# Issuing the experts' down pieces from ACT's own DMA queue instead of SP's

## The chip, the core and the metric

The program runs on one core of a Trainium2 chip. The metric is device microseconds of one execution, the median of three runs. The engines named here are PE (TensorE, matrix products), DVE (VectorE), ACT (ScalarE), POOL (GpSimd) and SP (SyncE, which in this kernel only issues transfers). A transfer is issued by an engine on its queue, is carried by the core's 16 DMA engines, and tells by a semaphore that it has landed.

## The reference

A two-layer trunk on 256 tokens of 1024 floats. Layer 0 is a hybrid attention and a dense SwiGLU, layer 1 is a latent attention and a mixture of experts. Only the last part matters here:

```python
def moe_swiglu(h, w_router, w_gu, w_down):
    logits = (h @ w_router).astype(jnp.float32)
    vals, idx = lax.top_k(logits, TOP_K)                      # TOP_K = 2
    gates = jax.nn.softmax(vals, axis=-1)
    combine = jnp.sum(jax.nn.one_hot(idx, N_EXPERTS) * gates[..., None], axis=-2)
    y = jnp.zeros_like(h)
    for e in range(N_EXPERTS):                                # 8 experts
        y = y + combine[..., e:e + 1] * swiglu(h, w_gu[e], w_down[e])
    return y
```

An expert has a gate-and-up matrix of 1024 x 7168 and a down matrix of 3584 x 1024, all float32: 44.04 MB, eight times.

## The kernel before

The first 480 us or so are layer 0, the attention of layer 1 and the router. From there on the eight experts follow one another, seven in a loop and the last written out again behind it.

**The pieces.** The weights of an expert come in 42 pieces of 1 MiB, 128 partitions by 2048 floats. The list `EXP` (line 102) gives the order in which PE uses them. Its numbers are used throughout: 0 to 7 gate and up of set 0, 8 to 15 gate and up of set 1, 16 to 19 down of set 0, 20 to 27 gate and up of set 2, 28 to 31 down of set 1, 32 to 35 gate and up of set 3 (each as two transfers of 512 KB), 36 to 39 down of set 2, 40 and 41 down of set 3. So 28 pieces are gate and up ("gu") and 14 are down ("d").

**The homes.** A piece lies in one of 14 buffers, the homes; piece i goes to home i mod 14. The piece that follows in a home may be loaded when PE has used the one before it. PE adds one to the semaphore `used` (printed as pieces_used) with its last matmul of each piece, so piece i may be issued once piece i-14 is used up. SP does this for all pieces in the order of the list: wait for `used`, issue, next (lines 438 to 446, `fill` at line 388).

**PE.** For each piece PE waits for the home's semaphore (line 1820) and runs 12 matmuls of 32 tokens columns by 512 (24 in the trace, since each is two passes): line 1831 for gu, line 1839 for d. Between pieces stand short steps: the scatter of the expert before after piece 7 (line 1772), transposes of the activations after pieces 11, 23, 33 and 39 (line 1797), and the gather of the next expert's tokens after piece 39 (line 1764).

**ACT.** Its work in an expert, in the order in which it is written (`expert`, line 879):

- set 0: three tanh (line 883) when the sums of the set are there, the copy of the scatter matrix (line 889, waits for the scatter), then two copies of transposed activations (line 861)
- sets 1 and 2: three tanh, two copies each
- set 3: three copies of odd rows (line 895), three tanh (line 898), one copy (861), two copies of gathered tokens (line 855), three copies of the outputs' odd rows (line 908)

DVE makes the activations out of ACT's tanh (lines 1403, 1407, and for set 3 1415 to 1425), and PE's transposes wait for DVE, its d matmuls for ACT's copies at line 861.

Of the kernel before, what the change touches and what calls it, by code (L numbers as in the profile page):

```python
# [33 lines left out]
NE, FFE = 8, 3584  # L34
# [52 lines left out]
SETS = 3  # L87
# [14 lines left out]
EXP = expert_order()  # L102
NU = len(EXP)
HOMES = 14
# [25 lines left out]
HOME_OF = [14] + [(U0 - RING + i) % RING for i in range(RING)]  # L130
# [30 lines left out]
def build(nc, A):  # L161
# [3 lines left out]
    with ctx:  # L165
# [15 lines left out]
        homes = placed("homes", [P, 15, PIECE], f32, 0)  # L181
# [92 lines left out]
        used = sem("pieces_used")  # L274
# [81 lines left out]
        def expert_source(e, piece):  # L356
            kind, k, c = piece
            if kind == "d":
                r = k * 1024 + c * 2 * P
                return A["l1_exp_w_down"][e, r:r + 2 * P, :].rearrange("(p j) n -> p (j n)", j=2)  # L360
            n0 = k * 1024
            if k < SETS:
                return A["l1_exp_w_gu"][e, c * P:(c + 1) * P, :].rearrange("p (h n) -> p h n", h=2)[:, :, n0:n0 + 1024]
            return A["l1_exp_w_gu"][e, c * P:(c + 1) * P, :].rearrange("p (h n) -> p h n", h=2)[:, :, n0:n0 + COLS]

        def per(value, e, step):

            return value if e is None else e * step + value
# [9 lines left out]
        @block.sync  # L378
        def _(sp):
            def load(u, src, n):  # L380
                if u >= RING:

                    sp.wait_ge(lo_ready, u - RING + 1)
                c = src.shape[1]
                dst = ring[:, u % RING, 0:n].rearrange("p (c n) -> p c n", c=c)
                sp.dma_start(dst, src).then_inc(ring_loaded[u % RING], 16)

            def fill(i, e):
                kind, k, c = EXP[i]
                dst, there = homes[:, HOME_OF[i % HOMES], :], home_loaded[i % HOMES]  # L390
                if kind == "d":
                    sp.dma_start(dst, expert_source(e, EXP[i])).then_inc(there, 16)
                elif k < SETS:
                    sp.dma_start(dst.rearrange("p (h n) -> p h n", h=2), expert_source(e, EXP[i])).then_inc(there, 16)
                else:
                    for j in range(2):
                        sp.dma_start(dst[:, j * 1024:(j + 1) * 1024].rearrange("p (h n) -> p h n", h=2),
                                     expert_source(e, (kind, k, 2 * c + j))).then_inc(there, 16)

            for t in range(NT):  # L400
                sp.dma_start(x[:, t, :], A["x"][0, t * P:(t + 1) * P, :]).then_inc(x_loaded[t], 16)
            sp.dma_start(gain, A["l0_norm_attn"].partition_broadcast(P)).then_inc(gain0_loaded, 16)
            sp.dma_start(ident[:, :], A["ident"]).then_inc(ident_loaded, 16)
            for u, piece in enumerate(STREAM):
                if u == SLOTS:

                    for k, name in enumerate(("l0_a_q_norm", "l0_a_k_norm", "l0_b_q_norm", "l0_b_k_norm")):
                        sp.dma_start(raw_gains[:, k, :], A[name].partition_broadcast(P)).then_inc(tab_in, 16)  # L408
                    for t in range(NT):
                        sp.dma_start(rope[:, t, :], A["rope"][t * P:(t + 1) * P, :]).then_inc(tab_in, 16)  # L410
                    sp.dma_start(arena3[:, D + 256:D + 512],
                                A["l0_a_lambda"].rearrange("k d -> (k d)").partition_broadcast(P)).then_inc(tab_in, 16)
                    sp.dma_start(subln[:, :], A["l0_a_subln"].partition_broadcast(P)).then_inc(early_loaded, 16)
                    sp.dma_start(sinks[:, 0, :], A["l0_b_sinks"].partition_broadcast(P)).then_inc(early_loaded, 16)
                    sp.dma_start(rw[:, :, :], A["l1_router"].rearrange("(c p) e -> p c e", p=P)).then_inc(early_loaded, 16)
                load(u, piece_source(piece), piece_floats(piece))

            def first_fill(i):

                if i == 0:  # L420
                    sp.wait_ge(used, first(FFN) + len(FFN))
                elif i <= RING:
                    sp.wait_ge(lo_ready, U0 - RING + i)
                elif i <= RING + 2 * SLOTS:
                    sp.wait_ge(used, U0 - SLOTS + (i - RING - 1) // 2 + 1)
                else:
                    sp.wait_ge(routed, 1)
                fill(i, 0)

            def expert_pass(p):  # L430
                ub = U0 + p * NE * NU
                for i in range(HOMES):
                    if p:
                        fill(i, 0)
                    else:
                        first_fill(i)
                with sp.Fori(0, NE - 1) as e:
                    for i in range(HOMES, NU):
                        sp.wait_ge(used, per(ub + i - HOMES + 1, e, NU))
                        fill(i, e)  # L440
                    for i in range(HOMES):
                        sp.wait_ge(used, per(ub + NU + i - HOMES + 1, e, NU))
                        fill(i, e + 1)
                for i in range(HOMES, NU):
                    sp.wait_ge(used, ub + (NE - 1) * NU + i - HOMES + 1)
                    fill(i, NE - 1)

            def store(p):

                for q in range(4):  # L450
                    t, c = q // 2, slice((q % 2) * COLS, (q % 2 + 1) * COLS)
                    sp.wait_ge(scat_added, 4 * (NE + 1) * p + 4 * NE + q + 1)
                    sp.dma_start(A["out"][0, t * P:(t + 1) * P, c], x[:, t, c]).then_inc(stored, 16)
                sp.wait_ge(stored, 64 * (p + 1))

            expert_pass(0)
            store(0)
            sp.wait_ge(flag_ready, 1)
            most = sp.value_load(nmax_i[0:1, 0:1], min_val=0, max_val=SEQ)
            with sp.If(most > CAP):  # L460
                for p in range(1, PASSES):
                    expert_pass(p)
                    store(p)
# [103 lines left out]
        def _(a):  # L567
# [281 lines left out]
            def expert_pass(p):  # L849
                ub = U0 + p * NE * NU  # L850
# [22 lines left out]
                for b in range(4):  # L873
# [2 lines left out]
                                 bank(SCAT_BANKS[b])[0:CAP, :].rearrange("p (e n) -> p e n", e=2), ACT.Copy)\  # L876
                        .then_inc(scat_ready, 1)

                def expert(e, last):
                    for k in range(SETS):  # L880
                        for g in range(NG):
                            set_done(k, g, EXP.index(("gu", k, KC - 1)), e)
                            a.activation(gate[0:64, g, :], PS[0:64, g, :], ACT.Tanh, scale=0.5)\  # L883
                                .then_inc(gate_ready, 1)
                        if k == 0:

                            a.wait_ge(scattered, per(4 + 4 * (NE + 1) * p, e, 4))
                            a.wait_ge(scat_ready, 4 * p + 4)
                            a.activation(scatT[0:CAP, :], scatT_all[0:CAP, bass.ds(e, 1), :]
                                         .rearrange("p e n -> p (e n)"), ACT.Copy).then_inc(scatT_ready, 1)  # L890
                        copy_acts(2 * k, e, aT_pair, 6)
                        copy_acts(2 * k + 1, e, aT_third, 7)
                    for g in range(NG):
                        set_done(SETS, g, EXP.index(("gu", SETS, KC // 2 - 1)), e)
                        a.activation(gate[0:64, g, :], PS[64:P, g, :], ACT.Copy).then_inc(odd_copied, 1)  # L895
                    for g in range(NG):
                        a.wait_ge(set3_added, per(NG * NE * p + g + 1, e, NG))
                        a.activation(aux[0:GROUP, g, :], gate[0:GROUP, g, :], ACT.Tanh, scale=0.5)\
                            .then_inc(gate_ready, 1)
                    copy_acts(6, e, aT_last, 6)  # L900
                    if not last:
                        copy_tokens(2, e)
                    for g in range(NG):
                        if g < NG - 1:
                            a.wait_ge(y_summed, per((NG - 1) * NE * p + g + 1, e, NG - 1))
                        else:
                            a.wait_ge(used, per(ub + NU, e, NU))
                        a.activation(aux[0:64, g, :], PS[64:P, 3 + g, :], ACT.Copy).then_inc(y_odd, 1)  # L908
# [1003 lines left out]
```

## Time and profile before

| | |
|---|---|
| median of three runs | 1481.71 us (1478.5 to 1482.38) |
| the profiled execution, its own time | 1483.62 us |
| span of the profiled execution | 1481.8 us |
| mean granted clock of TensorE | 0.971 |
| PE busy | 1397.7 us, 94% |
| ACT busy | 344.2 us, 23% |
| moved by DMA | 415.97 MB, mean 281 GB/s |
| d piece from issue to landing, median | 6.8 us |
| gu piece of 1 MiB from issue to landing, median | 6.7 us |

The span is the time from the first to the last instruction. A matmul that is counted busy is in the pipeline; its record says when PE could start it and not how much of the array it used. DMA's share is that of the core's 16 DMA engines.

### The profile page before, as it was taken

The numbers are of one execution on the slowest core, as the hardware profiler recorded it, in microseconds if no ns is written. First come the engines' busy times: TensorE is split into PE (matmuls) and PEld (weight loads), VectorE is DVE, ScalarE is ACT, GpSimd is POOL, SyncE is SP. The second block draws the span as 40 slices with busy tenths as digits, with TensorE's granted clock in tenths as the row PEclk, the third lists the DMA queues.
The fourth block names the chain that finished last, engine by engine and source line by source line (L and its number), as shares of the span: only waits on it lengthen the run. The fifth ranks groups of instructions, "written<-read, shape, count | busy, mean of one in ns | idle before, by whom it ended". The sixth has DMA issues, their size and how long they took to land.

```text
span 1481.8 us, 25123 instructions
## 1 busy us (share of the span) xinstructions
PE 1397.7 (94%) x10702; PEld 687.6 (46%) x10702; DVE 479.8 (32%) x691; ACT 344.2 (23%) x603; POOL 65.9 (4%) x116
## 2 busy tenths in 40 slices
PE   5888899998788999999999999999999999999997
PEld 5667688887677433333333333333333332333332
DVE  3865555555753211221211221122121122121213
ACT  4355434433672101110200110111020111111011
POOL 3300000003500000000000000000000000000000
PEclk9988999999998899999999999999999999999998
DMA  9404455545216599999999989999989998999960
GB/s 311 159 14 133 148 165 194 175 169 153 101 64 237 222 351 387 350 345 386 358 349 375 391 321 362 388 347 352 378 342 352 388 380 320 378 388 349 359 259 31
DMA packets 117167, 415.97 MB, mean 281 GB/s; under 512 B 9152, under 2 KB 13632, under 8 KB 102592
## 3 DMA queue, kind: packets, MB, share of 16 engines
q1 hardware_dynamic: 116384, 412.25, 74.5%
q0 software_dynamic: 672, 2.03, 0.6%
q8 instruction: 95, 1.56, 0.4%
q14 instruction: 16, 0.13, 0.0%
HBM read 413.21 MB, written 1.05 MB: 280 GB/s over the span
## 4 chain that ended last, share of the span: by engine, by line
PE 88%; DVE 4%; ACT 2%; issue 2%; POOL 1%; SPq 1%; DMA 1%; POOLq 0%; DVEq 0%; ACTq 0%
PE PS L1831 39%; PE PS L1839 19%; PE PS L1454 6%; PE PS L1456 6%; PE PS L1455 6%; PE PS L1797 2%; PE PS L1772 2%; PE PS L1764 2%; PE PS L1562 1%; PE PS L1520 1%; ACT arena L631 1%; POOL stat L483 1%; DMA arena<-in_l_a_lambda 1%; PE PS L1706 1%; SPq L408 1%
## 5 line engine op out<-in xcount | busy, mean ns | idle before, releaser
L1831 PE MATMUL PS<-homes,tabs 128*32 128x512 f32 x5376 | 588.0, 593 | 9.6 <-issue 8.1
L1831 PEld LDWEIGHTS PS<-homes,tabs 128*32 128x32 f32 x5376 | 172.3, 110 | 400.1 <-issue 393.2
L1839 PE MATMUL PS<-homes,arena 128*32 128x512 f32 x2688 | 294.4, 592 | 0.6 <-ACT arena L861 0.6
L1403 DVE SCALAR_TENSOR_TENSOR arena<-arena,PS 64x512 f32<-64x512 f32 x72 | 49.0, 680 | 529.5 <-ACT arena L883 528.8
L1839 PEld LDWEIGHTS PS<-homes,arena 128*32 128x32 f32 x2688 | 86.5, 110 | 197.7 <-issue 196.3
L936 DVE TENSOR_TENSOR w_lo<-ring,w_hi 128x2048 fp32r<-128x2048 f32 (+2 forms) x56 | 123.9, 2219 | 106.5 <-ACT w_hi L580 94.7
L1454 PE MATMUL PS<-w_hi,hT_hi 128*128 128x512 f32 (+2 forms) x372 | 144.8, 389 | 14.0 <-DVE w_lo L936 10.1
L1455 PE MATMUL PS<-w_lo,hT_hi 128*128 128x512 f32 (+2 forms) x372 | 142.7, 384 | 0.0
L1456 PE MATMUL PS<-w_hi,hT_lo 128*128 128x512 f32 (+2 forms) x372 | 142.5, 383 | 0.0
L861 ACT ACTIVATE arena<-PS 128x512 f32<-128x512 f32 (+2 forms) x56 | 27.5, 491 | 444.9 <-PE PS L1797 444.3
L580 ACT ACTIVATE w_hi<-ring 128x2048 fp32r<-128x2048 f32 (+2 forms) x56 | 103.8, 1859 | 94.5 <-PE PS L1456 94.4
L883 ACT ACTIVATE arena<-PS 64x512 f32<-64x512 f32 x72 | 42.6, 591 | 303.9 <-PE PS L1831 303.9
L1454 PEld LDWEIGHTS PS<-w_hi,hT_hi 128*128 128x128 f32 x372 | 72.5, 195 | 29.5 <-DVE w_lo L936 11.8
L1456 PEld LDWEIGHTS PS<-w_hi,hT_lo 128*128 128x128 f32 x372 | 72.3, 194 | 13.0
L1455 PEld LDWEIGHTS PS<-w_lo,hT_hi 128*128 128x128 f32 x372 | 72.6, 195 | 12.4
L1432 DVE TENSOR_TENSOR arena<-arena,PS 32x512 f32<-32x512 f32 x48 | 32.6, 679 | 104.3 <-ACT arena L908 103.0
L1415 DVE TENSOR_TENSOR arena<-arena,PS 64x512 f32<-64x512 f32 x24 | 16.3, 679 | 143.9 <-ACT arena L895 143.9
L1407 DVE SCALAR_TENSOR_TENSOR arena<-arena,PS 64x512 f32<-64x512 f32 x72 | 49.7, 690 | 2.2
L1797 PEld LDWEIGHTS PS<-ident,arena 128*128 128x128 f32 (+2 forms) x224 | 31.1, 211 | 29.7 <-issue 26.8
L483 POOL TENSOR_TENSOR stat<-stat,neg_half 128x1 f32<-128x1 f32 (+4 forms) x24 | 33.2, 1388 | 153.4 <-DVE stat L964 146.1
L1797 PE MATMUL PS<-ident,arena 128*128 128x128 f32 (+2 forms) x224 | 38.6, 301 | 0.0
L1772 PE MATMUL PS<-arena 96*128 96x512 f32 x72 | 35.0, 631 | 3.3 <-DVE arena L1432 3.3
(186 smaller groups left out, 903.4 us busy)
## 6 DMA issues: line engine op xcount, KB each, us to landing
homes<-in_l_exp_w_gu SPq DMA_DIRECT2D x192, 1024.0 KB, 6.7
homes<-in_l_exp_w_down SPq DMA_DIRECT2D x112, 1024.0 KB, 6.8
homes<-in_l_exp_w_gu SPq DMA_DIRECT2D x64, 512.0 KB, 6.2
ring<-in_l_ffn_w_gu SPq DMA_DIRECT2D x22, 1024.0 KB, 5.2
ring<-in_l_ffn_w_down SPq DMA_DIRECT2D x11, 1024.0 KB, 4.9
ring<-in_l_w_in SPq DMA_DIRECT2D x9, 1024.0 KB, 11.0
ring<-in_l_w_out SPq DMA_DIRECT2D x4, 1024.0 KB, 5.1
ring<-in_l_c_w_out SPq DMA_DIRECT2D x4, 1024.0 KB, 5.1
```

What stands on the lines that cost most here:

```text
L483: pool.tensor_tensor(s, s, neg_half[:, 0:R_COLS[r]], ALU.pow).then_inc(rstd_ready, 1)
L580: a.activation(w_hi[:, u % SLOTS, 0:n], ring[:, u % RING, 0:n], ACT.Copy).then_inc(hi_ready, 1)
L936: v.tensor_tensor(w_lo[:, u % SLOTS, 0:n], ring[:, u % RING, 0:n], w_hi[:, u % SLOTS, 0:n].bitcast(f32), ALU.subtract).then_inc(lo_ready, 1)
L1403: v.scalar_tensor_tensor(out=act_of[g], in0=gate[0:64, g, :], scalar=1.0, in1=PS[0:64, g, :], op0=ALU.add, op1=ALU.mult).then_inc(half_sil ...
L1407: v.scalar_tensor_tensor(out=act_of[g - 1], in0=act_of[g - 1], scalar=0.5, in1=PS[64:P, g - 1, :], op0=ALU.mult, op1=ALU.mult)\
L1454: pe.matmul(out, xh, wh, start=start, stop=False)
L1455: pe.matmul(out, xh, wl, start=False, stop=False)
L1456: return pe.matmul(out, xl, wh, start=False, stop=stop)
L1772: pe.matmul(bank(banks[q]), scatT[0:CAP, t * P:(t + 1) * P], y_exp[0:CAP, n * COLS:(n + 1) * COLS], start=True, stop=True).then_inc(scatte ...
L1797: ins = pe.transpose(bank(b)[:, j * m:(j + 1) * m], cols[:, j % 2, :], ident[0:m, 0:m])
L1831: ins = pe.matmul(PS[GROUP * q:GROUP * (q + 1), g, :], xT[:, cc, g * GROUP:(g + 1) * GROUP], w[:, q * COLS:(q + 1) * COLS], start=c == 0, ...
L1839: ins = pe.matmul(PS[GROUP * q:GROUP * (q + 1), 3 + g, :], tokens_T(k, c, q // 2, g), w[:, q * COLS:(q + 1) * COLS], start=k == 0 and c == ...
```

## The change

SP issues only the gu pieces. Each d piece is issued by ACT, in the midst of its own work, after a wait for the same value of `used` as before. ACT's issues stand at these places of an expert:

- place 1, after the copy of the scatter matrix of set 0: pieces 16, 17, 18, 19
- place 2, after the tanh of set 1: pieces 28, 29
- place 3, after the copies of set 1: pieces 30, 31, 36, 37
- place 4, after the tanh of set 2: pieces 38, 39
- place 5, after the copies of set 2: pieces 40, 41

```diff
             def fill(i, e):
...
-                if kind == "d":
-                    sp.dma_start(dst, expert_source(e, EXP[i])).then_inc(there, 16)
-                elif k < SETS:
+                if k < SETS:
...
                 with sp.Fori(0, NE - 1) as e:
                     for i in range(HOMES, NU):
-                        sp.wait_ge(used, per(ub + i - HOMES + 1, e, NU))
-                        fill(i, e)
+                        if EXP[i][0] == "gu":
+                            sp.wait_ge(used, per(ub + i - HOMES + 1, e, NU))
+                            fill(i, e)
...
                 for i in range(HOMES, NU):
-                    sp.wait_ge(used, ub + (NE - 1) * NU + i - HOMES + 1)
-                    fill(i, NE - 1)
+                    if EXP[i][0] == "gu":
+                        sp.wait_ge(used, ub + (NE - 1) * NU + i - HOMES + 1)
+                        fill(i, NE - 1)
...
+                def fill_down(k, cs, e):
+
+                    for c in cs:
+                        i = EXP.index(("d", k, c))
+                        a.wait_ge(used, per(ub + i - HOMES + 1, e, NU))
+                        a.dma_start(homes[:, HOME_OF[i % HOMES], :], expert_source(e, EXP[i]))\
+                            .then_inc(home_loaded[i % HOMES], 16)
+
                 def expert(e, last):
                     for k in range(SETS):
...
+                        fill_down(*((0, range(4)), (1, range(2)), (2, range(2, 4)))[k], e)
                         copy_acts(2 * k, e, aT_pair, 6)
                         copy_acts(2 * k + 1, e, aT_third, 7)
+                        if k == 1:
+                            fill_down(1, range(2, 4), e)
+                            fill_down(2, range(2), e)
+                        elif k == 2:
+                            fill_down(3, range(2), e)
```

**Place 1 on ACT.** L889 (L897 in the changed kernel) is the copy of the scatter matrix, L861 a copy of transposed activations. Before:

```order
L887 ISA
L889 ISA [waits scat_ready,scattered]
L889 ACTIVATE arena<-arena 96x256
L860 ISA
L861 ACTIVATE arena<-PS 128x512 [waits act_transposed]
```

In the changed kernel:

```order
L895 ISA
L897 ISA [waits scat_ready,scattered]
L897 ACTIVATE arena<-arena 96x256
L883 REGISTER_ALU
L884 ISA [waits pieces_used]
L884 DMA homes<-in_l_exp_w_down 128x2048
```

The last three rows stand there four times, once for each of pieces 16 to 19, and only then come the rows of L860 and L861.

**Place 5 on ACT.** The copies of set 2, and behind them the first copy of odd rows of set 3 (L895 before, L909 in the changed kernel). Before:

```order
L860 REGISTER_ALU
L861 ACTIVATE arena<-PS 128x512 [waits act_transposed]
L860 REGISTER_ALU
L861 ACTIVATE arena<-PS 128x256 [waits act_transposed]
L867 REGISTER_ALU
L895 ACTIVATE arena<-PS 64x512 [waits set_summed]
```

In the changed kernel:

```order
L861 ACTIVATE arena<-PS 128x256 [waits act_transposed]
L883 REGISTER_ALU
L884 ISA [waits pieces_used]
L884 DMA homes<-in_l_exp_w_down 128x2048
L884 ISA [waits pieces_used]
L884 DMA homes<-in_l_exp_w_down 128x2048
L867 REGISTER_ALU
L909 ACTIVATE arena<-PS 64x512 [waits set_summed]
```

Two issues, pieces 40 and 41, stand between the copies of set 2 and the first work of set 3.

**On SP, behind the gu pieces of set 3** (L397 before, L395 in the changed kernel). Before, d pieces (L392) follow:

```order
L397 ISA
L397 DMA homes<-in_l_exp_w_gu 128x2x512
L439 REGISTER_ALU
L392 ISA [waits pieces_used]
L392 DMA homes<-in_l_exp_w_down 128x2048
```

In the changed kernel SP goes on to piece 0 of the next expert:

```order
L395 ISA
L395 DMA homes<-in_l_exp_w_gu 128x2x512
L441 REGISTER_ALU
L392 ISA [waits pieces_used]
L392 DMA homes<-in_l_exp_w_gu 128x2x1024
```

The waits of the gu pieces themselves are the same as before; between them SP has nothing to issue while the d pieces are due.

## Rows read from the trace of the kernel before

**Rows 1.** The page: span, PE's busy time, DMA's busy tenths in 40 slices.

```profile
span 1481.8 us, 25123 instructions
...
PE 1397.7 (94%) x10702; PEld 687.6 (46%) x10702; DVE 479.8 (32%) x691; ACT 344.2 (23%) x603; POOL 65.9 (4%) x116
...
DMA  9404455545216599999999989999989998999960
```

**Rows 2.** Who PE waited for, 500 to 1480 us: total, times, longest.

```profile
PE PS L1831 <- issue: 8.1, 6, 1.5
PE PS L1772 <- DVE arena L1432: 3.3, 1, 3.3
PE PS L1839 <- ACT arena L861: 0.6, 1, 0.6
```

**Rows 3.** Timeline of PE in one expert: start, length, line, count.

```profile
1029.55 10.48 PE L1839 MATMUL PS<-homes,arena 128*32 128x512 f32 x96
1039.85 10.48 PE L1831 MATMUL PS<-homes,tabs 128*32 128x512 f32 x96
...
1061.89 10.48 PE L1839 MATMUL PS<-homes,arena 128*32 128x512 f32 x96
...
1083.92 10.48 PE L1839 MATMUL PS<-homes,arena 128*32 128x512 f32 x96
1094.34 0.72 PE L1797 MATMUL PS<-ident,arena 96*128 96x96 f32 x4
...
1098.56 5.36 PE L1839 MATMUL PS<-homes,arena 128*32 128x512 f32 x48
```

**Rows 4.** Timeline of SP's issues in the same expert.

```profile
991.24 8.06 SPq L392 DMA_DIRECT2D homes<-in_l_exp_w_down  x4
1001.54 23.78 SPq L394 DMA_DIRECT2D homes<-in_l_exp_w_gu  x8
1027.35 8.06 SPq L392 DMA_DIRECT2D homes<-in_l_exp_w_down  x4
...
1047.95 14.66 SPq L392 DMA_DIRECT2D homes<-in_l_exp_w_down  x6
1064.86 46.69 SPq L394 DMA_DIRECT2D homes<-in_l_exp_w_gu  x16
```

**Rows 5.** Timeline of ACT in the same expert; in brackets its idle time before.

```profile
1007.70 0.42 ACT L889 ACTIVATE arena<-arena 96x256 f32 x1 [3.12 <-PE PS L1772]
1018.71 1.01 ACT L861 ACTIVATE arena<-PS 128x512 f32<-128x512 f32 x2 [10.59 <-PE PS L1797]
...
1029.80 0.59 ACT L883 ACTIVATE arena<-PS 64x512 f32<-64x512 f32 x1 [0.27 <-PE PS L1831]
1051.05 1.01 ACT L861 ACTIVATE arena<-PS 128x512 f32<-128x512 f32 x2 [20.66 <-PE PS L1797]
1060.42 0.59 ACT L883 ACTIVATE arena<-PS 64x512 f32<-64x512 f32 x1 [8.37 <-PE PS L1831]
...
1078.23 1.01 ACT L861 ACTIVATE arena<-PS 128x512 f32<-128x512 f32 x2 [15.51 <-PE PS L1797]
1082.46 0.59 ACT L895 ACTIVATE arena<-PS 64x512 f32<-64x512 f32 x1 [3.22 <-PE PS L1831]
```

**Rows 6.** Timeline of DVE: its last work on the activations of set 3.

```profile
1088.25 1.40 DVE L1425 SCALAR_TENSOR_TENSOR arena<-arena 32x512 f32<-32x512 f32 x2
```

**Rows 7.** Busy time by window; the last two numbers are DMA's share and GB/s.

```profile
462.00:474.00 12.00, 8.99 (x45) 7.55 (x44) 6.31 (x10) 4.58 (x8) 1.13 (x2) 0.85 1.02 410
...
991.24:1113.58 122.34, 120.81 (x1080) 41.26 (x1076) 24.94 (x37) 15.28 (x28) 0.00 (x0) 1.00 0.94 361
```

**Rows 8.** Line 392 (d pieces), length of one issue in ns, min/median/max.

```profile
L392 SPq DMA_DIRECT2D homes<-in_l_exp_w_down x112: 327/333/374, 502.8 to 1427.2; - x112
```

**Rows 9.** Line 386, transfers of mostly 1 MiB issued one by one, 30 to 330 us.

```profile
DMA to landing us min/median/max: 3.6/5.0/6.7
```

**Rows 10.** Timeline of SP in the first 5 us: an issue that took long.

```profile
2.61 1.66 SPq L386 DMA_DIRECT2D ring<-in_l_w_in  x3
4.32 6.00 SPq L408 DMA_DIRECT2D arena<-in_l_a_q_norm  x1
```

## The prediction

> **What bounds the kernel now.** I read the page first. PE is busy for 94% of a span of 1481.8 us, ACT for 23%, and from the 15th of the 40 slices on DMA stands at 8 or 9 tenths nearly throughout [rows 1]. Two resources are near their limit in the stage that the change touches, so the question is which of them makes the other wait. The list of PE's waits answers it: in the 980 us of the experts PE was idle for 8.1 us at "issue", once 3.3 us for DVE and once 0.6 us for ACT, and never for a transfer [rows 2]. The timeline says the same as a rhythm. Pieces 16 to 19 start at 1029.55 and piece 20 at 1039.85 [rows 3], so one piece takes 10.30 / 4 = 2.575 us. SP's four issues of down pieces lie over 8.06 us, three steps and the last issue of 0.33 us: (8.06 - 0.33) / 3 = 2.58 us [rows 4, 8]. SP thus issues at PE's pace, whenever PE has let go of a home. One expert takes 122.34 us, from 991.24 to 1113.58, at a granted clock of 1.00 [rows 7].
>
> How near is DMA? An expert is 42 pieces, 44.04 MB, in 122.34 us: 360 GB/s, and the window shows 361 at a share of 0.94 [rows 7]. What DMA could do has two bounds: 361 / 0.94 = 384 GB/s if the share is taken at its word, and 410 GB/s, which the burst of first pieces reached [rows 7]. One piece of 1.049 MB then costs DMA 2.73 or 2.56 us, and an expert 114.7 or 107.5 of its 122.3 us. DMA has 8 to 15 us to spare in each expert. A transfer issued one by one takes 5.0 us to land [rows 9], so about 2.4 us of that are not transport.
>
> **The change, part by part.**
>
> *SP loses 14 issues per expert.* They lay in waits for PE. The gu pieces keep their waits and their times. Worth 0.
>
> *ACT gains 14 issues per expert.* One costs 0.333 us on SP [rows 8]; with the register step and the wait ahead of it I take 0.45 us, so 6.3 us per expert and 50 us of ACT in all. It is hidden if it fits ACT's idle times. Place 1: ACT is free at 1008.12 and its next work is at 1018.71, 10.59 us for four issues of 1.8 us [rows 5]. Place 2: from 1030.39 to 1051.05. Place 3: from 1052.06 to 1060.42, 8.37 us for 1.8 us. Place 4: the tanh of set 2 begin at 1060.42 and are 0.86 us apart, so the third ends at 1062.73; the next work is at 1078.23. Place 5 is the narrow one: from 1079.24 to 1082.46, 3.22 us for two issues of 0.9 us [rows 5]. All fit. Cost 0.
>
> *The waits that go with them.* A wait for `used` on ACT would hold up the tanh and the copies queued behind it, and DVE and PE behind those. The value for piece i is i-13 pieces of the expert used. At place 1, ACT stands behind the scatter, which follows piece 7: at least 8 used, and 3 to 6 asked. At place 2 ACT has just waited for 16, and 15 and 16 are asked. Place 3 follows transposes behind piece 23: 24 used, asked 17, 18, 23, 24. Place 4: 28 used, asked 25, 26. Place 5: 34 used, asked 27, 28. No wait ever blocks. Cost 0.
>
> *The d pieces start later.* This is the term on which everything rests, since PE waits for the home if a piece lands late. I take the issue as 0.1 us after ACT is free and let the two queues share DMA evenly, at 2 x 2.56 = 5.1 us for each of ACT's pieces, plus 2.4 us. That is harsh, since SP doesn't always have a transfer. PE's needs are the starts in [rows 3] and steps of 2.575 us.
>
> - Place 1 (16 to 19), issued from 1008.2: landed at 1015.7, 1020.8, 1025.9, 1031.0; needed at 1029.6, 1032.1, 1034.7, 1037.3. Least slack 6.3 us.
> - Place 2 (28, 29), from 1030.5: landed by 1043; needed at 1061.9 and 1064.5. Slack 21 us.
> - Place 3 (30, 31, 36, 37), from 1052.2: landed at 1059.7, 1064.8, 1069.9, 1075.0; needed at 1067.0, 1069.6, 1083.9, 1086.5. Least slack 4.8 us, and here SP has nothing in hand between the last gu piece of set 3, issued before 1047.95, and 1064.86 [rows 4], so the true one is larger.
> - Places 4 and 5 (38 to 41), queued behind piece 37 at 5.1 us each: 1080, 1085, 1090, 1095; needed at 1089.1, 1091.6, 1098.6, 1101.1. Least slack 6.1 us.
>
> With 2.73 us for a piece instead of 2.56 the four of place 1 land at 1032.4 at the latest, and 31 at 1065.5: still in time. Nothing stalls. Cost 0.
>
> *DMA stands idle where it did not.* SP's last gu piece before place 1 is issued one step before 991.24, the next at 1001.54, where now four d pieces go out [rows 4]. With landing at 6 to 7 us, DMA will stand still for roughly 6 to 8 us. Before, it had 8 to 15 us to spare per expert, and what is postponed is served while the burst of place 1 queues behind SP's stream. This turns spare time round and takes none from PE. Cost 0.
>
> *A second queue.* Whatever its setup costs lies at the start or in the 1.8 us between the span and the execution's own time of 1483.62 us. No row prices it; between 0 and 2 us, and I take 0.
>
> **The sum** is 1483.6 + 0 for the profiled execution, and that execution was 1.9 us over the median of the runs. Against the median: 1481.7 us. A gain is not to be had from the change either, since PE waits for nothing that it touches.
>
> **The Trainium skill** speaks against this room at one point. The trace shows 410 GB/s in a burst and 361 GB/s over a whole expert [rows 7]. "DMA: Bandwidth & Descriptors" (section "Where 436 GB/s comes from") says that for transfers from HBM to SBUF the limit is the core's share of HBM, about 358 GB/s. By that rule the 44.04 MB take 123.0 us, more than the 122.34 us of an expert, and the sum would be 0.7 us x 8 = 5 us more. The trace doesn't agree with the rule for this core; its figure is the mild case of rival B.
>
> **Rivals.**
>
> *A. The ACT queue gets less than an even share.* No row has two busy queues, so sharing isn't shown. The bound on this side is that SP's transfers always go first. SP's stream at one piece per 2.575 us fills DMA at 2.56 us a piece. Then pieces 16 to 19 go out only when SP pauses: SP's last of eight is issued near 1024.8 [rows 4], DMA is free at 1027.3, and they land from about 1030.8 on, 1.2 us late. Piece 39, issued at 1063, is starved by the stream from 1064.86, until PE stops at 1091.6, which stops SP too; three pieces in flight end near 1094.6, and 39 lands near 1098.6, 7 us late. That is 8 x 1.2 + 7 x 7 = 59 us: 1541 us. It decides from the point where the fourth piece of place 1 comes after 1037.3: (1037.3 - 1008.2 - 2.4) / 4 = 6.7 us a piece, a share under 38%. For it speaks only that nothing excludes it. The rule of the same page ("Queues, rings and completion order") is that a DMA engine takes turns between its queues packet by packet, which is the even share; no row shows it.
>
> *B. Two queues make DMA slower.* If mixing two streams costs rate, DMA falls behind PE below 360 GB/s, 6% under the 384 and 12% under the 410. At 358 GB/s an expert takes 123.0 us, 0.7 us more, in all 5 us: 1487 us. At 346 GB/s it takes 127.3 us, 5 us x 8 = 40 us more: 1522 us, which I take as its price. The traffic of each queue is of the same size of piece as before, which speaks against it.
>
> *C. An issue blocks ACT.* One issue of SP took 6.00 us, behind seven transfers issued within 4 us [rows 10]. If a burst does that to ACT at place 5, the copies of set 3 come at 1079.24 + 0.9 + 6.0 = 1086.1 instead of 1082.46, 3.7 us late. DVE ends that set at 1089.65 [rows 6] and PE transposes it at 1094.34 [rows 3], so 4.7 us of cover hides even this. At 10 us of blocking 3 us x 8 = 24 us show: 1506 us.
>
> *D. Faster.* The only idle time of PE that something like fetching of instructions could explain is the 8.1 us at "issue" [rows 2]. Less traffic at that moment might shorten it; all of it gone gives 1473.6 us.
>
> **How the numbers follow.** The forecast, no change: 0.86. A 0.05, B 0.04, C with a visible price 0.02, D 0.03. A difference of over 0.3%, 4.4 us, is about what a measurement can tell from no change. So faster 0.03, same 0.86, slower 0.11. The range for 8 in 10 is the scatter of the runs before, 1478.5 to 1482.4, widened by the setup of 0 to 2 us and by small lateness: 1477 to 1488.
>
> **What the profile will show.** ACT has 112 issues of about 0.33 us and none of SP's for d pieces. Landing of d pieces grows from 6.8 us to a median of 9 to 13 us and a longest one near 20. SP's gu issues keep their times, DMA's windows show a hole of several us ahead of place 1, PE's list of waits has no transfer in it, and an expert still takes 122.3 us. An entry of PE at lines 1831 or 1839 that ends with a landing says A or B: only d pieces late is A, a lower GB/s at a full share is B. ACT issues longer than 1 us say C. The forecast is wrong if any of these lasts over 0.6 us per expert.

## The result, and the profile after

The changed kernel takes 1503.3 us, median of three runs (1501.44 to 1504.14), against 1481.71 us: a ratio of 1.0149, 95% interval 1.0122 to 1.0176. It is slower by 21.6 us, where no change was forecast and slower by over 0.3% had a chance of 0.11. The profiled execution took 1501.44 us, 1.8 us over its span, as before, so no setup of a second queue shows there.

The page after, the lines that answer to [rows 1], and the queues, where q10 is ACT's:

```profile
span 1499.6 us, 25111 instructions
...
PE 1401.3 (93%) x10702; PEld 683.5 (46%) x10702; DVE 479.8 (32%) x691; ACT 343.7 (23%) x603; POOL 67.2 (4%) x116
...
DMA  9404455546125599699979969969997996997962
...
q1 hardware_dynamic: 100256, 294.81, 52.3%
q10 hardware_dynamic: 16128, 117.45, 19.5%
...
homes<-in_l_exp_w_gu SPq DMA_DIRECT2D x192, 1024.0 KB, 11.9
homes<-in_l_exp_w_down ACTq DMA_DIRECT2D x112, 1024.0 KB, 8.8
```

DMA's row of the stage of the experts now has dips to 6 and 7, about one per expert: the idle stretch that was foreseen ahead of place 1. And the gu pieces, whose issues nobody touched, take 11.9 us to land instead of 6.7 (medians of those of 1 MiB). That second number is the trail.

Who PE waited for, 490 to 1500 us (total, times, longest), the stage that [rows 2] shows of the kernel before:

```profile
PE PS L1845 <- issue: 22.4, 6, 3.8
PE PS L1786 <- DVE arena L1446: 3.3, 1, 3.3
PE PS L1853 <- ACT arena L861: 0.6, 1, 0.6
```

Still no wait that ends with a transfer. Only the six waits at "issue" have grown, from 8.1 to 22.4 us. The timeline of PE shows where one of them lies, between the last matmuls of an expert (line 1853) and the first of the next (1845):

```profile
1107.86 5.36 PE L1853 MATMUL PS<-homes,arena 128*32 128x512 f32 x48
1117.02 7.48 PE L1845 MATMUL PS<-homes,tabs 128*32 128x512 f32 x52 [3.80 <-issue]
```

This is where PE's loop over seven experts turns. There are six turns; the way into the last expert, which is written out behind the loop, has none and shows no wait. In the kernel before, the same place of the same expert reads

```profile
1098.56 5.36 PE L1839 MATMUL PS<-homes,arena 128*32 128x512 f32 x48
1105.45 7.07 PE L1831 MATMUL PS<-homes,tabs 128*32 128x512 f32 x64 [1.53 <-issue]
```

From start to start that is 6.89 us before and 9.16 us after. I call the time from the start of PE's last matmul ahead of a turn to its next one the gap. It was 1.69 to 2.13 us at the six turns before and is 4.01 to 4.43 us after. The way from one turn to the next I call a cycle.

The windows tell what DMA does meanwhile. The columns are the stretch, its length, the busy time of PE, weight loads, DVE, ACT and POOL, then granted clock, DMA share and GB/s. Before, the last matmuls ahead of the turn and the gap:

```profile
1098.56:1103.33 4.77, 4.77 (x49) 1.46 (x48) 0.43 (x1) 1.29 (x3) 0.00 (x0) 1.00 0.32 94
1103.33:1105.45 2.12, 0.59 (x8) 0.01 (x1) 2.03 (x4) 0.98 (x2) 0.00 (x0) 1.00 0.88 323
```

After, the same two stretches, and the 3.43 us behind the gap:

```profile
1107.86:1112.63 4.77, 4.77 (x49) 1.46 (x48) 0.43 (x1) 1.28 (x3) 0.00 (x0) 1.00 1.03 410
1112.63:1117.02 4.39, 0.59 (x9) 0.01 (x1) 3.64 (x6) 0.99 (x2) 0.00 (x0) 1.00 1.02 407
...
1117.02:1120.45 3.43, 3.43 (x20) 0.89 (x24) 0.00 (x0) 0.00 (x0) 0.00 (x0) 0.51 0.71 279
```

Before, DMA was two thirds idle when PE came to its turn (0.32, 94 GB/s): PE's transposes and its gather after piece 39 release no home, so SP issues nothing and the queue drains. After, DMA runs at its full 410 GB/s. And behind the gap PE's granted clock is 0.51, the lower of its two levels (1.2 instead of 2.4 GHz); it had been idle for most of 4.39 us before that. Behind the same gap of the kernel before (1105.45 to 1108.88) the clock is 1.00. The clock was low behind five of the six turns after, and behind none before.

From the first matmul on an expert's piece to the last, the stage took 970.8 us before (from 494.66) and 993.2 us after (from 489.28). The difference of 22.4 us has two parts: the waits at "issue", 22.4 - 8.1 = 14.3 us, and PE's busy time at line 1845, 596.2 us against 588.0 at line 1831, 8.2 us, that is five times about 1.65 us at half the clock. (The stage ahead of the experts was 5.4 us shorter in this execution than in the one before, which is why the spans differ by 17.8 us; the medians differ by 21.6.)

**Theory T.** Something that PE needs at its turn is carried by the same 16 DMA engines as the weights, and comes late when they are busy with weights. The records of DMA packets name it: a packet of 16384 bytes on the queue for instructions (q8). Before, this packet starts 0.59 to 1.10 us ahead of the start of PE's last matmul; after, 1.18 to 1.56 us behind it. PE's next matmul follows the packet's start by 2.7 to 3.2 us in both, and at the turns of all the experiments below that have any. The record doesn't say which engine a packet is for; that this one is PE's is read from that constant distance. The Trainium skill, "Runtime: NRT & Kernel Launch", section "Instruction fetch mechanics", says that a taken branch to a page that isn't at hand forces a DMA fetch of that page before execution can go on, in blocks of 16 KiB; the trace agrees, with these packets. That the fetch waits behind weights it doesn't say.

**Rivals.** Q: a second queue costs by itself. L: down pieces that come late hold PE. P: what counts is the last burst of down pieces ahead of the turn, pieces 40 and 41.

### The profile page after: what moved, and what is told of

Read it like the earlier page. It is cut to its first block, busy times and chain, and to the rows that moved or that the text cites. A ratio compares the mean times of both kernels' runs of the same rounds, so it can differ in the third digit from the quotient of the medians.

```text
span 1499.6 us, 25111 instructions
## 1 busy us (share of the span) xinstructions
PE 1401.3 (93%) x10702; PEld 683.5 (46%) x10702; DVE 479.8 (32%) x691; ACT 343.7 (23%) x603; POOL 67.2 (4%) x116
## 3 DMA queue, kind: packets, MB, share of 16 engines
q8 instruction: 95, 1.56, 0.4%
## 4 chain that ended last, share of the span: by engine, by line
PE 87%; DVE 4%; issue 3%; ACT 2%; POOL 2%; SPq 1%; DMA 0%; POOLq 0%; DVEq 0%; ACTq 0%
PE PS L1845 39%; PE PS L1853 19%; PE PS L1468 6%; PE PS L1469 6%; PE PS L1470 6%; PE PS L1811 2%; PE PS L1786 2%; PE PS L1778 2%; PE PS L1576 1%; ACT arena L631 1%; PE PS L1534 1%; POOL stat L483 1%; SPq L406 1%; PE PS L1720 1%; ACT tabs L644 0%
## 5 line engine op out<-in xcount | busy, mean ns | idle before, releaser
L1845 PE MATMUL PS<-homes,tabs 128*32 128x512 f32 x5376 | 596.2, 599 | 23.7 <-issue 22.4
L861 ACT ACTIVATE arena<-PS 128x512 f32<-128x512 f32 (+2 forms) x56 | 27.4, 490 | 444.9 <-PE PS L1811 444.3
L1470 PEld LDWEIGHTS PS<-w_hi,hT_lo 128*128 128x128 f32 x372 | 71.7, 193 | 12.8
L1469 PEld LDWEIGHTS PS<-w_lo,hT_hi 128*128 128x128 f32 x372 | 71.9, 193 | 12.1
## 6 DMA issues: line engine op xcount, KB each, us to landing
homes<-in_l_exp_w_gu SPq DMA_DIRECT2D x192, 1024.0 KB, 11.9
ring<-in_l_w_in SPq DMA_DIRECT2D x9, 1024.0 KB, 11.9
```

What stands on the lines that cost most here:

```text
L1469: pe.matmul(out, xh, wl, start=False, stop=False)
L1470: return pe.matmul(out, xl, wh, start=False, stop=stop)
L1845: ins = pe.matmul(PS[GROUP * q:GROUP * (q + 1), g, :], xT[:, cc, g * GROUP:(g + 1) * GROUP], w[:, q * COLS:(q + 1) * COLS], start=c == 0, ...
```

## The experiments

Each kernel was measured beside the kernel before on the same chip. A ratio is to that, with its 95% interval. A diff is to the changed kernel, or to the kernel before where the expectation says so, and lines left out of it are marked with dots. "In time" means issued when the home comes free, "late" as late as in the changed kernel.

### The same queue, issued in time

```diff
                     for k in range(SETS):
+                        if k == 0:
+                            fill_down(0, range(4), e)
                         for g in range(NG):
...
-                        fill_down(*((0, range(4)), (1, range(2)), (2, range(2, 4)))[k], e)
+                        if k == 1:
+                            fill_down(1, range(4), e)
+                            fill_down(2, range(1), e)
+                        elif k == 2:
+                            fill_down(3, range(2), e)
                         copy_acts(2 * k, e, aT_pair, 6)
                         copy_acts(2 * k + 1, e, aT_third, 7)
                         if k == 1:
-                            fill_down(1, range(2, 4), e)
-                            fill_down(2, range(2), e)
-                        elif k == 2:
-                            fill_down(3, range(2), e)
+                            fill_down(2, range(1, 4), e)
```

> The down pieces stay on ACT's queue, but each is issued when its home comes free, as SP did before: 16 to 19 ahead of the tanh of set 0, 28 to 31 and 36 behind the tanh of set 1, 37 to 39 behind the copies of set 1, 40 and 41 behind the tanh of set 2. ACT then waits inside its own idle times. Theory T (lateness makes a backlog of transfers that is still there when PE turns its loop; PE's next instructions come late, PE stands still longer, and its clock falls): no backlog at the turn, so the gap of PE at the six turns is near 2.0 us as before, the granted clock never 0.5 there, the cycle 122.2 us, the time that of before within 4 us (about 1482). Rival Q (a second queue costs by itself, wherever the issues stand): the cycle stays near 126 us and the time near 1503.

Measured: 1480.12 us against 1481.01, ratio 0.9993 (0.9982 to 1.0003). The whole loss is gone with ACT still issuing all 112 down pieces. PE's waits, and the last 4.77 us ahead of the start of PE's last matmul, the window that had a DMA share of 0.32 before:

```profile
PE PS L1848 <- issue: 7.5, 6, 1.7
```

```profile
1096.46:1101.23 4.77, 4.77 (x49) 1.46 (x48) 0.43 (x1) 1.28 (x3) 0.00 (x0) 1.00 0.38 130
```

Q falls: the second queue costs nothing that can be measured. ACT's waits for `used`, which now really block it, cost nothing either: in the expert looked at they lie in its idle time, 8.07 us of issues ahead of the tanh of set 0 and 18.29 us behind those of set 1.

### One queue, issued late

```diff
+                late = {21: (8, (16, 17, 18, 19)), 27: (16, (28, 29)), 35: (24, (30, 31, 36, 37)),
+                        NU - 1: (28, (38, 39)), NU + 4: (34, (40, 41))}
+
+                def fill_after(i, e):
+                    if i in late:
+                        count, pieces = late[i]
+                        sp.wait_ge(used, per(ub + count, e, NU))
+                        for j in pieces:
+                            fill(j, e)
```

`fill_after` is called behind each gu piece of SP; ACT issues nothing.

> All transfers on SP's one queue as in the kernel before, but the down pieces are issued as late as the changed kernel does: 16 to 19 when 8 pieces of the expert are used, 28 and 29 at 16, 30, 31, 36, 37 at 24, 38 and 39 at 28, 40 and 41 at 34. Theory T: the backlog at the loop's turn is there with one queue too, so the gap of PE is 4 us or more at the six turns, the cycle near 126 us, the time near 1503. Rival Q (the second queue is the cause): cycle 122.2 us, time 1482.

Measured: 1501.73 us, ratio 1.0129 (1.0108 to 1.015). The gap at the turns is 3.94 to 4.17 us, the clock low behind four of them.

```profile
PE PS L1846 <- issue: 20.7, 6, 3.6
```

```profile
1111.08:1115.85 4.77, 4.77 (x48) 1.46 (x48) 0.43 (x1) 1.28 (x3) 0.00 (x0) 1.00 1.02 407
```

With the experiment before it this settles which half of the change matters: lateness without the second queue gives nearly the whole loss, the second queue without lateness gives none.

### Nothing late, but a backlog at the turn

```diff
                         fill(i, e + 1)
+                        if p == 0 and i == 5:
+                            for j in range(2):
+                                sp.wait_ge(extra[j], per(16, e, 16))
+                                load_extra(j)
```

`load_extra` loads part of a down matrix into memory that nothing uses in this stage. A first pair of such loads is issued ahead of SP's loop.

> The kernel before, plus two loads per turn that nobody reads, 1 MiB and 0.9 MB, issued by SP behind piece 5 of the next expert, the place where the changed kernel has pieces 40 and 41 put into the stream. They make a backlog of some two pieces (landing 11 to 12 us instead of 6.5) in front of the loop's turn; all real pieces are still issued at their old times. Theory T: the gap of PE at the six turns grows from 2.0 to about 4.3 us, the clock drops there, the cycle is near 126 us, the time near 1504. Rival L (PE waits for down pieces that are late): no down piece is late here, so 1482.

Measured: 1496.15 us, ratio 1.0097 (1.0073 to 1.0121): two thirds of the loss, where all of it was expected. The six gaps are 2.87 to 4.37 us, and the instruction packets start 0.02 to 1.54 us behind PE's last matmul, the later the longer the gap. The clock is low behind three turns; a cycle with it takes 125.5 to 126.3 us, one without it 123.1 to 123.7.

```profile
PE PS L1845 <- issue: 18.3, 6, 3.8
```

L falls: here every real piece is issued at its old time: counted from the scatter of an expert, SP's issues up to the turn lie within 0.11 us of those of the kernel before. What came out smaller fits a smaller backlog: the gu pieces issued within 12 us ahead of a turn took 11.1 to 12.4 us to land at the worst, where the changed kernel has 12.2 to 12.4 at every turn.

### The changed kernel with the queue drained at the turn

```diff
                     for i in range(HOMES):
-                        sp.wait_ge(used, per(ub + NU + i - HOMES + 1, e, NU))
+                        sp.wait_ge(used, per(ub + NU + (1 if i > 8 else i - HOMES + 1), e, NU))
                         fill(i, e + 1)
```

> The changed kernel, with SP holding back pieces 9 to 13 of the next expert until PE has used that expert's piece 0, so that nothing is in flight when PE turns its loop; the pieces are needed 20 us later. Theory T: gap at the turns back to about 2 us or less, no drop of the clock, time near 1482. Rivals Q and L (second queue as such, late down pieces): the lateness and the queue are unchanged, time near 1503.

Measured: 1480.65 us, ratio 0.9992 (0.9982 to 1.0003), gaps of 1.61 to 2.21 us, no low clock. Five pieces are issued later still than in the changed kernel, and all of the loss is gone.

```profile
PE PS L1845 <- issue: 7.8, 6, 1.6
```

```profile
1096.03:1100.80 4.77, 4.77 (x49) 1.46 (x48) 0.43 (x1) 1.29 (x3) 0.00 (x0) 1.00 0.02 5
```

DMA is idle ahead of the turn (0.02, 5 GB/s), and this buys nothing over the share of 0.32 of the kernel before: the gap does not fall below 1.6 us. The median landing of the gu pieces of 1 MiB is 12.1 us here, without any loss: what matters is the backlog at the turn and not over the expert.

### Which lateness

The four pieces of place 1 alone:

> Down pieces on ACT's queue, pieces 16 to 19 as late as in the changed kernel (behind the scatter), the other ten when their homes come free. Theory T (what counts is the backlog of transfers when PE turns its loop): a burst 90 us ahead of the turn has been served by then, gap about 2 us, no drop of the clock, time about 1481. If every lateness adds its share, a good part of the 21 us stays: 1490 or more.

Measured: 1483.7 us against 1482.79, ratio 1.0002 (0.9991 to 1.0013), gaps 1.69 to 2.05 us. The other ten alone:

> Down pieces on ACT's queue, pieces 16 to 19 when their homes come free, the other ten as late as in the changed kernel. Theory T: the whole loss is here, gap 4.3 us at the turns with the clock at 0.5 behind most of them, time about 1502. If every lateness adds its share: about 1490 to 1495.

Measured: 1504.36 us, ratio 1.0138 (1.0115 to 1.0162), gaps 4.01 to 4.43 us, five low clocks. The loss isn't spread over the places: place 1 has none of it, the rest has all. The windows ahead of the turn, first with place 1 late, then with the rest late:

```profile
1099.38:1104.15 4.77, 4.77 (x48) 1.46 (x48) 0.43 (x1) 1.28 (x3) 0.00 (x0) 1.00 0.83 289
```

```profile
1111.77:1116.54 4.77, 4.77 (x48) 1.46 (x48) 0.43 (x1) 1.28 (x3) 0.00 (x0) 1.00 1.02 407
```

A share of 0.83 is harmless. DMA may still be busy ahead of the turn, as long as it comes to the end of what is queued.

The idle stretch ahead of place 1 that the prediction foresaw is there in the harmless kernel and missing in the costly one. The 7 us that end 3.16 us ahead of the scatter, first with place 1 late, then with the rest late:

```profile
994.52:1001.52 7.00, 7.00 (x68) 2.16 (x64) 0.00 (x0) 0.00 (x0) 0.00 (x0) 1.00 0.00 0
```

```profile
1006.91:1013.91 7.00, 7.00 (x68) 2.16 (x64) 0.00 (x0) 0.00 (x0) 0.00 (x0) 1.00 0.99 349
```

What the late ten add is idle time further on. In the 14 us that start 46 us behind the scatter, around place 3, DMA's share is 1.00 before, 1.03 with place 1 late, 0.88 in the changed kernel and 0.84 with the rest late. Whatever is not moved there is still to be moved when SP's long stream of gu pieces starts, and that stream leaves no room for it.

### Two pieces near the turn

```diff
+                        if k == 2:
+                            fill_down(3, range(2), e)
                         copy_acts(2 * k, e, aT_pair, 6)
                         copy_acts(2 * k + 1, e, aT_third, 7)
...
-                        elif k == 2:
-                            fill_down(3, range(2), e)
```

> The changed kernel, with its last two issues (40, 41) 17 us earlier, behind 38 and 39 at place 4. Theory T: the loop's turn comes 23 us after place 5, but SP's stream of gate and up pieces leaves DMA no room to serve what is queued (one piece per 2.575 us, served in about 2.56), so the backlog at the turn is the same: gap about 4.2 us, time about 1503. Rival P (the burst nearest to the turn is what delays it): gap and time fall clearly, to 1490 or less.

Measured: 1504.7 us against 1482.09, ratio 1.0147 (1.0126 to 1.0168), gaps 4.01 to 4.37 us, DMA at 1.03 and 410 GB/s ahead of the turn. Rival P falls: issuing the last pair 17 us earlier returns nothing. That fits SP's stream of one piece per 2.575 us, which leaves DMA, at 2.56 us a piece, no time to work off what is queued.

The converse, all in time but pieces 40 and 41:

> Down pieces on ACT's queue when their homes come free, only 40 and 41 as late as in the changed kernel (place 5). Theory T: two pieces of backlog on top of the 6.5 us of landing before, 11 to 12 us at the turn, gap 3 to 4.3 us, time 1493 to 1503. If it takes the whole lateness of ten pieces to make the backlog, the time is near 1482.

Measured: 1485.08 us (1479.58 to 1490.99 over ten runs), ratio 1.003 (1.0011 to 1.005), gaps 2.18 to 2.29 us in the profiled execution, no low clock. The expectation of 1493 to 1503 was wrong. The profiled execution, at 1483.42 us, is one of the faster ones; what the turns of the two at 1490 to 1491 us were like isn't shown.

```profile
PE PS L1848 <- issue: 9.8, 6, 1.7
```

```profile
1096.93:1101.70 4.77, 4.77 (x49) 1.46 (x48) 0.43 (x1) 1.28 (x3) 0.00 (x0) 1.00 0.98 366
```

The share is 0.98, and that is the edge. The last microsecond ahead of the start of PE's last matmul tells the two apart, first here, then in the changed kernel:

```profile
1100.70:1101.70 1.00, 1.00 (x16) 0.26 (x8) 0.43 (x1) 0.73 (x2) 0.00 (x0) 1.00 0.81 193
```

```profile
1111.63:1112.63 1.00, 1.00 (x16) 0.26 (x8) 0.43 (x1) 0.73 (x2) 0.00 (x0) 1.00 1.02 410
```

With only the last pair late DMA moves half its rate there, since it runs out of weights, and in this microsecond the instruction packet starts, 0.63 to 0.71 us ahead of PE's last matmul. The gu pieces issued within 12 us ahead of this turn took up to 6.7 us to land before, 10.3 us here and 12.4 us in the changed kernel. At 2.56 us a piece that is, by my estimate, 1.4 pieces more in the queue here and 2.2 there. PE releases nothing while it transposes and gathers after piece 39, 4.2 us from 1094.34 to 1098.56 in [rows 3], and that is the time in which DMA can catch up: 1.4 pieces are 3.6 us and fit into the pause, 2.2 are 5.6 us and don't.

### No turn at all

```diff
-                with pe.Fori(0, NE - 1) as e:
-                    expert(e, False)
+                if p == 0:
+                    for e in range(NE - 1):
+                        expert(e, False)
+                else:
+                    with pe.Fori(0, NE - 1) as e:
+                        expert(e, False)
                 expert(NE - 1, True)
```

Made to the changed kernel:

> The changed kernel, with PE's program for the first seven experts written out in place of its loop (the other engines keep theirs), so that PE has no turn. Theory T: a turn costs 126.2 - 120.6 = 5.6 us in the changed kernel, six of them 33.6 us; the backlog of transfers is the same and costs nothing, cycle 120.6 us throughout, time 1503.3 - 33.6 = about 1470. If the loss is due to late pieces or to transfers disturbing PE in another way, the time stays well above that of the same edit made to the kernel before.

Measured: 1472.15 us against 1482.79, ratio 0.993 (0.9907 to 0.9953). And to the kernel before:

> The kernel before, with the same edit. A turn costs 122.2 - 120.6 = 1.6 us there, six of them 9.6 us: time about 1481.4 - 9.6 = 1472. Theory T: within 3 us of the changed kernel with the same edit, since the two differ only by what a turn costs.

Measured: 1472.56 us, ratio 0.9932 (0.991 to 0.9954). Every one of the first seven experts takes 120.59 us in both, and neither has a wait of PE at "issue" or a low clock behind an expert in the stage. The queue for instructions carries 86 packets where the kernels with the loop have 95. Of the changed kernel with this edit, PE's list of waits from its longest on, and the page's DMA issues:

```profile
PE PS L1786 <- DVE arena L1446: 3.3, 1, 3.3
PE PS L1853 <- ACT arena L861: 0.6, 1, 0.6
```

```profile
homes<-in_l_exp_w_gu SPq DMA_DIRECT2D x192, 1024.0 KB, 11.9
homes<-in_l_exp_w_down ACTq DMA_DIRECT2D x112, 1024.0 KB, 8.7
```

The backlog is all there, 11.9 us of landing, and it costs nothing. With the turn taken away the two kernels differ by 0.4 us, within the scatter of either, so the whole effect of the change goes through the turn. Both are faster than the kernel before, by about 0.7%: 10.2 us, where six turns at 1.6 us are 9.6. A turn costs 122.2 - 120.6 = 1.6 us with a drained DMA and 126.2 - 120.6 = 5.6 us with a backlog and a low clock behind it.

The DMA share in this table is that of the last 4.77 us ahead of PE's last matmul, at one turn of each kernel.

| kernel | ratio | issue waits of PE, us | gaps, us | turns with low clock | DMA share ahead of the turn |
|---|---|---|---|---|---|
| before | 1 | 8.1 | 1.69 to 2.13 | 0 | 0.32 |
| changed | 1.0149 | 22.4 | 4.01 to 4.43 | 5 | 1.03 |
| ACT, in time | 0.9993 | 7.5 | 1.61 to 2.25 | 0 | 0.38 |
| SP, late | 1.0129 | 20.7 | 3.94 to 4.17 | 4 | 1.02 |
| before, two loads more | 1.0097 | 18.3 | 2.87 to 4.37 | 3 | 1.03 |
| changed, SP holds five | 0.9992 | 7.8 | 1.61 to 2.21 | 0 | 0.02 |
| place 1 late | 1.0002 | 8.0 | 1.69 to 2.05 | 0 | 0.83 |
| the rest late | 1.0138 | 21.5 | 4.01 to 4.43 | 5 | 1.02 |
| last pair at place 4 | 1.0147 | 21.5 | 4.01 to 4.37 | 5 | 1.03 |
| only last pair late | 1.003 | 9.8 | 2.18 to 2.29 | 0 | 0.98 |
| changed, PE written out | 0.993 | 0 | none | none | |
| before, PE written out | 0.9932 | 0 | none | none | |

## Why the prediction was wrong, point by point

*What bounds the kernel.* Right: PE, at 2.575 us a piece. The six waits at "issue" of [rows 2] were read and set aside as a possible gain (rival D). They were the place of the loss.

*14 issues on ACT.* Right. Line 884 from 1015 to 1090 us, the 14 issues of one expert:

```profile
L884 ACTq DMA_DIRECT2D homes<-in_l_exp_w_down x14: 339/339/912, 1017.2 to 1088.9; - x14
...
DMA to landing us min/median/max: 4.8/8.8/14.6
```

The median is 0.34 us, all fit ACT's idle times, and at the narrow place 5 ACT reaches its next work with the same 3.22 us of idle time as in [rows 5]. The longest issue of the whole run is 1.43 us, over the 1 us that was named as the sign of rival C, but it held up nothing that shows: rival C did not come with a price.

*No wait blocks.* Right: the issues follow ACT's work at once, 1017.22 behind the copy of 1017.00.

*The d pieces start later and still come in time.* Right in sign, too harsh in size. At place 1 the four landed 4.8, 8.8, 12.8 and 16.5 us after the first issue, where 7.5, 12.6, 17.7 and 22.8 were worked out. The d pieces took about 3.9 us each instead of 5.1, so ACT's queue had more than its half while both were full; no rival A. The prediction took turns packet by packet for an even share, and no row priced it. The records show what it is in bytes: from 1021 to 1033 us there start 401 packets of 8192 bytes on ACT's queue and 417 of 4096 bytes on SP's, so nearly as many packets and twice the bytes (274 against 142 GB/s with the small ones). Over the whole run the median landing of d pieces is 8.8 us, just under the 9 to 13 that were forecast, and the longest 15.2 us, where one near 20 was. With pieces 40 and 41 in flight beside SP's stream, DMA moved what one queue did in [rows 7]; no rival B, not in its mild case of 5 us either:

```profile
1088.00:1104.00 16.00, 16.00 (x149) 4.94 (x148) 6.05 (x9) 3.85 (x8) 0.00 (x0) 1.00 1.02 413
```

*DMA stands idle where it did not, cost 0.* **This is the step that failed.** The idle stretch is there: from 1003 to 1010 us DMA moved nothing.

```profile
1003.00:1010.00 7.00, 7.00 (x68) 2.13 (x64) 0.00 (x0) 0.00 (x0) 0.00 (x0) 1.00 0.00 0
```

And this stretch by itself did cost nothing: the kernel with place 1 late has it too, at 1483.7 us. What failed is the conclusion, "turns spare time round and takes none from PE", together with its premise that one idle stretch per expert is all that the change makes. The other ten pieces were checked only for being there in time, which they are, and nobody asked what their lateness does to DMA. DMA's spare time before was not spread evenly: some of it lay where PE makes its transposes, its gather and its turn, with a share of 0.32 over the last 4.77 us ahead of PE's last matmul. With the ten pieces late this stretch is full (1.02 and 1.03), and there DMA has another customer, PE's own instructions: 14.3 us of longer gaps and 8.2 us of low clock. I had the shares per window and looked at the mean of 0.94 only. The forecast of landing named the d pieces; gu pieces at 11.9 us would have shown the backlog standing over the whole of SP's stream, to its very end at the turn.

*The clock.* The sum took 1.00 for granted. Eight of the 22 us are the low clock behind five turns, a cost that no turn with a gap up to 3.47 us had in any kernel here.

*Rival D* had the right mechanism, the fetch of instructions, with the sign turned round: with less traffic ahead of the turn the waits hardly shrink (7.5 and 7.8 against 8.1 us), with more they grow to 22.4. Its 1473.6 us for all of them gone is near the 1472.6 us of the kernel with the turn written out.

*The signs.* "PE's list of waits has no transfer in it" came true and said nothing, since the late packet shows as "issue". The expert of 122.3 us became one of 126.3 us, and none of the entries that were named as signs of A and B appeared.

## What to carry to other kernels

Where DMA is nearly full, moving a transfer in time moves DMA's idle stretches too; look which work besides the data sits in the stretch that fills up, above all an engine's loop that turns there. Here each turn of PE's loop cost 1.6 us even with DMA drained. So keep the queues drained ahead of such a turn, or write the loop out on that one engine: that gave 0.7% and made this kernel indifferent to when weights are issued. Whether a shorter loop body would have such a turn wasn't tried. And when a transfer that was not touched takes nearly twice as long to land, there is a backlog, even if nobody waits for its data. Look where it stands: 11.9 and 12.1 us cost nothing without a turn, or with DMA drained ahead of it.

## What was not expected of the hardware

- A packet with instructions comes late when DMA is full of weights. It starts 0.02 to 1.56 us behind the start of PE's last matmul with DMA at 407 to 411 GB/s, and 0.4 to 1.1 us ahead of it where DMA has run dry by then. That it stands in line behind the weights is an inference: its request is not recorded, and so neither is how long it waited.
- The effect sets in late and steeply. With a share of 0.83 ahead of the turn there is none, at 0.98 it is 0.3%, at 1.02 to 1.03 it is 1.0 to 1.5%.
- The granted clock fell to half behind 22 of the 30 turns of the five kernels in which it fell at all. A gap of 3.55 us had it and two of 4.43 us hadn't, so the gap's length alone does not decide. Of the five gaps over 3.5 us without it four are the first of their kernel; what decides stays open.
- One queue and two queues move the same 407 to 413 GB/s, and a d piece of 1 MiB costs ACT a median of 0.34 us to issue, as it did SP. With both queues full the split was not even: ACT's pieces landed 3.9 us apart, SP's in the same stretch took 12.6 to 13.7 us each. The counts of packets above go with turns packet by packet, and d pieces come in packets twice as large. No experiment changed their size.
